# A hybrid decoder layer on one core: scan banks per kind, and steps of the planner moved

## The reference

```python
# A: gated DeltaNet, 4 heads x 128: short convolution, silu, chunked delta rule
qkv = silu(short_conv([q_a, k_a, v_a], conv_w))
v_new = u_i - w_i @ state
o     = q_i @ state + a_i @ v_new
state = state * gl + k_i.T @ v_new
# B: 4 heads x 64 over a latent of 128; a ReLU indexer of 8 heads selects 256 keys
score = sum_j relu(q_idx_j @ k_idx) * w_j ;  idx = top_k(score, 256)
p     = softmax(q_abs @ c[idx] * 64**-0.5 - slope * dist)
# C: cross-attention, 4 heads x 64, into 256 memory tokens
p_m   = softmax(q_m @ k_m * 64**-0.5) ;  o_m = p_m @ v_m
y     = concat(rmsnorm(o_a) * silu(z_a), o_s * silu(z_s), o_m * silu(z_m)) @ w_out
x     = layernorm(2**0.25 * x + y)
```

## Time and profile before

| what | us |
|---|---|
| median of 3 runs (780.77 to 781.71) | 781.16 |
| profiled execution | 782.2 |
| its span | 780.4 |
| PE busy | 712.9 (91%) |
| DVE busy | 483.9 (62%) |
| ACT busy | 452.2 (58%) |
| POOL busy | 181.7 (23%) |

### The profile page before, as it was taken

How to read it: one execution, slowest core, us unless ns; L and a number is a source line. 1 busy time by engine, 2 the same in 40 slices (tenths; PEclk the granted TensorE clock), 3 DMA queues, 4 the chain that set the end, 5 groups by cost and what they waited for, 6 DMA issues and landing times.

```text
span 780.4 us, 11927 instructions
## 1 busy us (share of the span) xinstructions
PE 712.9 (91%) x4204; PEld 591.0 (76%) x4204; DVE 483.9 (62%) x1076; ACT 452.2 (58%) x1027; POOL 181.7 (23%) x272
## 2 busy tenths in 40 slices
PE   6999999989999999999999989998777989899994
PEld 4887888778788888887888778876566767686773
DVE  5532888966756757563755658686644465654643
ACT  5522777787869987799959962223752242423410
POOL 0000000045102621136102431010365343143330
PEclk9999999999999999999999999999978999999998
DMA  9411020122300340023300252010961231332101
GB/s 356 133 68 63 19 95 29 40 72 63 120 28 29 92 136 28 28 72 89 122 28 28 85 142 83 28 47 33 333 181 40 75 115 47 109 97 74 68 28 55
DMA packets 63915, 65.90 MB, mean 84 GB/s; under 512 B 16368, under 2 KB 49392, under 8 KB 63472
## 3 DMA queue, kind: packets, MB, share of 16 engines
q1 hardware_dynamic: 63856, 65.13, 25.7%
HBM read 48.35 MB, written 16.78 MB: 83 GB/s over the span
## 4 chain that ended last, share of the span: by engine, by line
PE 63%; DVE 13%; ACT 11%; issue 9%; POOL 2%; DMA 2%; SPq 0%; ACTq 0%; DVEq 0%; POOLq 0%
PE bank L1054 10%; PE bank L1056 10%; PE bank L1055 10%; ACT cst L1938 4%; PE bank L1046 4%; PE bank L1408 4%; PE bank L1060 3%; PE bank L1409 3%; PE bank L1410 3%; DVE score L1534 2%; PE bank L1350 2%; PE bank L1240 2%; PE bank L1238 2%; PE bank L1219 2%; POOL w_out_lo L2194 2%
## 5 line engine op out<-in xcount | busy, mean ns | idle before, releaser
L1054 PE MATMUL bank<-x_hi,ring_split 128*128 128x512 f32 x480 | 197.1, 411 | 8.3 <-DVE x_lo L1483 7.3
L1056 PE MATMUL bank<-x_hi,ring_split 128*128 128x512 f32 x480 | 188.4, 393 | 0.0
L1055 PE MATMUL bank<-x_lo,ring_split 128*128 128x512 f32 x480 | 187.9, 392 | 0.0
L1938 ACT ACTIVATE cst<-score,sel 128x896 bf16<-128x896 f32 (+3 forms) x192 | 167.1, 873 | 25.7 <-DVE sel L1556 23.6
L1054 PEld LDWEIGHTS bank<-x_hi,ring_split 128*128 128x128 f32 x480 | 90.8, 189 | 25.3 <-DVE ring_split L1487 7.8
L1056 PEld LDWEIGHTS bank<-x_hi,ring_split 128*128 128x128 f32 x480 | 90.5, 189 | 19.8
L1055 PEld LDWEIGHTS bank<-x_lo,ring_split 128*128 128x128 f32 x480 | 90.9, 189 | 15.0
L1855 ACT ACTIVATE arena<-bank 128x512 f32<-128x512 f32 (+1 forms) x69 | 37.4, 563 | 55.7 <-PE bank L1060 48.6
L2125 POOL TENSOR_TENSOR arena<-arena,hsc 128x512 f32<-128x512 f32 x8 | 8.3, 1039 | 259.4 <-ACT arena L2008 259.4
L1408 PE MATMUL bank<-w_out_hi,mix_hi 128*128 128x512 f32 x128 | 54.4, 425 | 11.4 <-DVE mix_lo L1801 7.8
L2112 POOL TENSOR_TENSOR arena<-arena,cst 128x512 f32<-128x512 f32 x24 | 33.3, 1409 | 92.9 <-PE bank L1219 50.3
(11 more groups left out here) (288 smaller groups left out, 1400.9 us busy)
## 6 DMA issues: line engine op xcount, KB each, us to landing
ring<-in_w_groups SPq DMA_DIRECT2D x30, 512.0 KB, 3.4
x_raw<-in_x_t SPq DMA_DIRECT2D x8, 512.0 KB, 9.3
side_z<-stage SPq DMA_DIRECT2D x16, 256.0 KB, 2.0
w_out_sb<-in_wout_t SPq DMA_DIRECT2D x2, 2048.0 KB, 11.5
zgT<-side_z SPq DMA_DIRECT2D x8, 512.0 KB, 4.5
qkvT<-in_x SPq DMA_DIRECT2D x8, 512.0 KB, 3.4
out_y<-arena SPq DMA_DIRECT2D x8, 512.0 KB, 3.0
ring<-in_wmem_t SPq DMA_DIRECT2D x2, 1024.0 KB, 4.7
```

The source lines that it names most:

```text
L1054: nc.tensor.matmul(dst, hi, xh, start=(c == 0), stop=False)
L1055: nc.tensor.matmul(dst, hi, xl, start=False, stop=False)
L1056: last = nc.tensor.matmul(dst, lo, xh, start=False, stop=(c == KT - 1))
L1938: sc.activation(signs[order[e] % 2][:, 0:w], score[:, score_at(b):score_at(b + 1)], ACT.Sign, scale=-1.0, bias=candidate[:, b - 2:b - 1], ...
```

## The change

It is made in the planner and in the table of PSUM pools; beside them only the convolution is cut in two.

- Pools: V has bank 4, S bank 5, the outputs (R) banks 6 and 7. Other tiles of pool D still take the banks 4 to 7 in turn.
- Convolutions: a `conv` step does two of the four taps, and the second half stands one unit later, or at the start of the next list of units.
- The preparation of head 0: `KBT` stands one unit later, the product two, `latent_scale` and `base` one in the list of shares.
- Attention blocks: `norms` leaves the middle of a block and stands directly ahead of `memory`. `msc` of the next block stands one place earlier in its list, from the second block on. `mix_split(b, 1)` stands directly behind `mixT(b, 1)`, with empty units behind both.

```diff
--- before.py
+++ after.py
@@ -187,8 +187,11 @@
         units[1] = [*second, *units[1]]
         units[3] = [*fourth, *units[3]]
         if part < 2:
-            units[3].append(("conv", h, part, 0))
-            units[7].append(("conv", h, part, 1))
+            units[3].append(("conv", h, part, 0, 0))
+            units[4].append(("conv", h, part, 0, 1))
+            units[7].append(("conv", h, part, 1, 0))
+        if part == 0:
+            units[0].append(("conv", h, 1, 1, 1))
         return units
 
     def value_part(h, rest):
@@ -198,7 +201,7 @@
 
     def head(h, rest):
 
-        return [*part_of(h, 1), *part_of(h, 0, [("silu", h, 1)]), [("silu", h, 0)], *value_part(h, rest)]
+        return [*part_of(h, 1), *part_of(h, 0, [("silu", h, 1)]), [("conv", h, 0, 1, 1), ("silu", h, 0)], *value_part(h, rest)]
 
 
     side = [[("side", g, t, s)] for g in range(N_SIDE) for t in range(2) for s in range(4)]
@@ -210,7 +213,7 @@
     queries[0].append(("gate_values",))
     queries[3] += [("tok", 0, a, 1) for a in range(2)]
     queries[6].append(("ksum", 0))
-    first_work = [*keys, [("kmT",)], [("gates",)], *queries, [("gate_sums",)], [("vm",)], [("silu", 0, 0)], []]
+    first_work = [*keys, [("kmT",)], [("gates",)], *queries, [("conv", 0, 0, 1, 1), ("gate_sums",)], [("vm",)], [("silu", 0, 0)], []]
     n_units = len(first_work)
     index_tiles = [("idx", b, j, c) for b in range(2, NB) for c in range(len(idx_chunks(b))) for j in range(IXH)]
     for i, e in enumerate(index_tiles):
@@ -280,7 +283,7 @@
     def product(h):
         return [*pair("U", h), ("diag_out", h)]
 
-    ahead = [*pair("GB", 0), 1, ("KB", 0, 0), ("KB", 0, 1), 1, 1, *pair("KBT", 0), 1, 1, *product(0), *[1] * 5, ("latent_scale",), ("base", 0), *[1] * 6, ("diag_back", 0), 2]
+    ahead = [*pair("GB", 0), 1, ("KB", 0, 0), ("KB", 0, 1), 1, 1, 1, *pair("KBT", 0), 1, 1, 1, *product(0), *[1] * 4, ("latent_scale",), ("base", 0), *[1] * 5, ("diag_back", 0), 2]
     woven(ahead, value_part(0, side[:N_SIDE_AHEAD]))
     side = side[N_SIDE_AHEAD:]
     for h in range(DNH):
@@ -330,7 +333,6 @@
         units = [[("mpT", b, 0)], [("mpT", b, 1)], *[[("pT", b, k)] for k in range(b + 1)]]
         units[min(3, b + 2)].append(("rinv", b))
         units += [[] for _ in range(max(0, 5 - len(units)))]
-        units[min(5, len(units) - 1)].append(("norms", b))
         for j in range(b // 2):
             units[min(2 * j + 5, len(units) - 1)].append(("weighted", b, j))
         return units
@@ -339,6 +341,8 @@
 
         s0 = 2 * i
         pieces = [[("y", b, c, s0 + s)] for c in range(2) for s in range(2)]
+        if i:
+            return [[("mixT", b, i), ("mix_split", b, i)], [], [], [], [], *pieces]
         return [[("mixT", b, i)], [("mix_split", b, i)], [], [], *pieces]
 
     def merged(*queues):
@@ -362,13 +366,13 @@
         if nb is not None:
             at = [scores(nb, h) for h in range(SAH)]
             at[1] = [*at[1], *([("qsplit", BLOCK_ORDER[n + 2])] if n + 2 < NB else [])]
-            place = 3 if n else 4
+            place = 2 if n else 4
             at[place:place] = [[("msc", nb, 0), ("msc", nb, 1)]]
             queues.append((0.5, at))
         if n == 1:
             before = half_out(prev, 0)
             after = half_out(prev, 1)
-            out = [*before[:2], *after[:2], *[[("y", prev, c, s)] for c in range(2) for s in range(4)]]
+            out = [*before[:2], after[0], [], *[[("y", prev, c, s)] for c in range(2) for s in range(4)]]
         elif n:
             out = half_out(prev, 1)
         else:
@@ -393,6 +397,7 @@
         for unit in held[:1]:
             for e in unit:
                 add(e)
+        add(("norms", b))
         add(("memory", b))
         add(("weighted", b, b // 2))
         if n == 0:
@@ -405,7 +410,7 @@
     assert plan.index(("scanS", DNH - 2, NB - 1)) < plan.index(("reach", 7))
     assert plan.index(("At", DNH - 1, 1)) < plan.index(("dm", SELECT_ORDER[0], 1))
     assert plan.index(("tok", DNH - 1, 1, 2)) < plan.index(("dm", SELECT_ORDER[0], 2))
-    assert all(plan.index(("At", h - 1, 1)) < plan.index(("conv", h, 1, 0)) for h in range(1, DNH))
+    assert all(plan.index(("At", h - 1, 1)) < plan.index(("conv", h, 1, 0, 0)) for h in range(1, DNH))
     assert all(plan.index(("silu", h, 1)) < plan.index(("tok", h, 0, 1)) for h in range(DNH))
     return with_splits(plan)
 
@@ -478,9 +483,9 @@
     if k == "y":
         return [("Y", e[:3])] if e[3] == 0 else []
     if k == "scanV":
-        return [("D", ("V", e[1], e[2]))]
+        return [("V", ("V", e[1], e[2]))]
     if k == "scanS":
-        return [("D", ("S", e[1], e[2]))] * (e[2] < NB - 1) + [("D", ("O", e[1], e[2]))]
+        return [("S", ("S", e[1], e[2]))] * (e[2] < NB - 1) + [("R", ("O", e[1], e[2]))]
     if k == "tok":
         return [("L" if e[3] == 1 else "D", e)]
     return [(POOL_OF[k], e)] if k in POOL_OF else []
@@ -703,7 +708,7 @@
         bst, mv, rstd, ealog = hsc[:, 0:12], hsc[:, 12:14], hsc[:, 14:15], misc[:, 52:56]
         ss_k, ln_k, rs_k, f_kb, f_kd = (hsc[:, 16 + 8 * i:24 + 8 * i] for i in range(5))
 
-        pools = {"P": (0, 1), "L": (2, 3), "D": (4, 5, 6, 7), "A": (4, 5, 6), "O": (0,), "Y": (1, 7)}
+        pools = {"P": (0, 1), "L": (2, 3), "D": (4, 5, 6, 7), "V": (4,), "S": (5,), "R": (6, 7), "A": (4, 5, 6), "O": (0,), "Y": (1, 7)}
         banks = [ctx.enter_context(nc.psum_tensor(f"bank{i}", [P, 512], F32)) for i in range(8)]
         filled_sem = [sem(f"filled{i}") for i in range(8)]
         released_sem = [sem(f"released{i}") for i in range(8)]
@@ -1629,16 +1634,16 @@
                                                       ALU.mult, ALU.subtract)
                     last.then_inc(release_of(e), 1)
                 elif k == "conv":
-                    h, part, t = e[1:]
-
-                    dve.wait_ge(*released(("proj", h, part, t)))
-                    if (h, part, t) == (0, 1, 0):
-                        dve.wait_ge(cw_sem, 16)
-                    if t == 0 and part == 0 and h > 1:
-                        dve.wait_ge(*filled(("O", h - 2, NB - 1)))
-                    if t == 0 and part == 1 and h:
-                        dve.wait_ge(*filled(("At", h - 1, 1)))
-                    for j in range(4):
+                    h, part, t, half = e[1:]
+                    if half == 0:
+                        dve.wait_ge(*released(("proj", h, part, t)))
+                        if (h, part, t) == (0, 1, 0):
+                            dve.wait_ge(cw_sem, 16)
+                        if t == 0 and part == 0 and h > 1:
+                            dve.wait_ge(*filled(("O", h - 2, NB - 1)))
+                        if t == 0 and part == 1 and h:
+                            dve.wait_ge(*filled(("At", h - 1, 1)))
+                    for j in (2 * half, 2 * half + 1):
                         conv_tap(h, part, t, j)
                 elif k == "tap":
                     h, t, j = e[1:]
```

## The result

The changed kernel takes **775.82 us** (median of 4, 775.74 to 777.49) against 781.43 (median of 4) for the kernel before: a ratio of 0.9928, 95% interval 0.9914 to 0.9942. The forecast was 771.9 in a range of 764.9 to 778.0: the sign and the range held, but of the 9.3 us forecast only 5.6 came. The profiled execution's span is 774.1 us, 6.3 less than before.

What follows compares the result with a forecast made beforehand. PE was taken to bound the kernel (63% of the last-ending chain), with only its idle waits to win. Terms 1.2 + 0.7 + 0.5 - 1.1 + 2.0 + 3.3 + 2.75 - 0.1 = 9.25 us gave 771.9 us, range 764.9 to 778.0.

Steps and rivals of the forecast that it cites:

- Banks per kind, the sites: Scans: V no longer waits for the outputs' addition, 0.52 us a site; 0.5 in head 0, none in heads 1, 2.
- At(2,1): Second attention tile of head 2 waits for its new bank, last used by head 1's outputs: a loss of 1.1 us.
- Key products: Head 0 before the first scan: products a point on, latent scaling after the taps; gain 1.2 us, between 0 and 2.6.
- Convolutions: Halved, two taps go behind M's subtraction at 214 us: gain 0.7 us; nothing in later heads or during index scores.
- The whole to 466 us: Key products 1.2, convolutions 0.7 and head 0's bank site 0.5, less 1.1 at At(2,1): 1.3 us net.
- Block 3 and head 3: Norms at the first block's end (1.5 us or more) and head 3's scan (1.7), capped together by a side load: 2.0 us.
- Block 4: Second block: earlier memory scores fill the wait for POOL's low weights, norms at the end; gain 3.3 us.
- Blocks 2, 5, 1, 6, 0, 7: Same edits in later blocks, against DVE's queue: gains 1.8, 1.8, -0.9, 1.25, -1.2 and 0, sum +2.75 us.
- the neighbours: Low half directly behind the gate: saves output-product waits but delays score maxima where two-chunk blocks follow; sum -0.1 us.
- The low clock: After longer waits in blocks 1 and 0, PE's clock falls from 614 to 770 us: up to 786 us; chance 0.06.
- Rival B: The key search absorbs the first half's gains, 2.4 us less: 774.3 us; chance 0.10.

Runs made afterwards that it cites:

- experiment 8: Changed kernel with head 0's key products, latent scaling and base chain back at their old places: 778.8 us, ratio 0.9947 to the kernel before.
- experiment 5: The changed kernel run once more, unaltered, as reference of its group: 777.2 us, ratio 0.9934 to the kernel before.
- experiment 3: Changed kernel with the attention blocks ordered as before; only scan banks, key products and convolutions remain: 781.6 us, ratio 0.9994.
- experiment 9: Changed kernel with the memory scores of the next block at their old place: 783.0 us, ratio 1.0018.
- experiment 10: Changed kernel with norms in the middle of each block as before: 774.5 us, ratio 0.9906.
- experiment 7: Changed kernel with another bank for At(2,1); for blocks 1 and 0, memory scores at their old place and the preceding block's gate and low half apart: 775.2 us.
- experiment 12: Kernel of experiment 11 with head 0's key products back at their old places: 773.3 us, ratio 0.9899.
- experiment 4: Changed kernel with gate and low half apart again, as before: 778.3 us, ratio 0.9943.
- experiment 6: Changed kernel with At(2,1) of head 2 in bank 5 and not 7, second run of that kernel: 777.8 us, ratio 0.9943.
- experiment 11: Kernel of experiment 7 with norms of blocks 1 and 0 in the middle again, these two blocks wholly as before: 772.9 us, ratio 0.9887.
- experiment 2: Kernel before with the attention blocks' edits alone: 779.8 us, ratio 0.9965.

## Why the prediction was right, and where its sizes were off

- **Banks per kind, the sites.** In each scan of heads 0 to 2 the ladder wins 0.4 us and loses it again by the next head's M or first copies: 0.1 lasts in head 0, where I counted 0.5 (mis-sized), and nothing in heads 1 and 2, as forecast. Head 3: 1.7 forecast, 1.3 by the ladder (+1.6 to +0.3).
- **At(2,1).** The mechanism and the place were right, the term was mis-sized: 1.1 us forecast, 1.7 measured, of which 1.4 last. I had worked it out from PE's position in the kernel before, 1.1 us ahead of the release. The release moves with PE, but not by all of it: the 0.4 us that the banks win in the scan just ahead bring PE on and not the addition, which ended 1.4 us earlier where PE was 1.8 earlier. 1.1 and 0.4 are the 1.5 us of all seven profiles; the rest lies between the end of the addition (370.08) and PE's start (370.23).
- **Key products.** 1.2 us forecast, 1.4 measured (+1.1 at 159 us to -0.3 at 200; experiment 8 gives 1.5). Right, and for the reason given: 2.1 us won by 188, and the rest taken back by the search, at 195 us already and not at 206. The base chain came late in no profile: no M waited for it.
- **Convolutions.** This step failed. The 0.7 us at M came (0.9, -0.3 to -1.2), but I had put the halves at nothing while the index scores run, "the same work in another order", and they cost 0.8 us there. Before 123 us DVE had room for those taps without holding PE; a few microseconds later ACT and then PE wait for it. That the sum of DVE's work stays the same says nothing on that, and I had not looked at where DVE had room. Net 0.1 in place of 0.7.
- The whole to 466 us: forecast 1.3 us net. Measured 0.3 behind from the loads, 1.4 and 0.1 won, 0.1 in head 0's scan, 1.4 lost at At(2,1): a loss of 0.1 us, 0 by the ladder.
- **Block 3 and head 3.** 2.0 forecast; 2.7 in this trace from 470 to the last product of block 3, 2.2 in experiment 5. Head 3's scan gives 1.3 of it. Norms at the end gives nothing (experiments 3, 9 and 10). From 551 us to y(3,0,0) experiment 3, whose blocks stand in the order of before, wins 0.9 us as well: in the profile of the kernel before the clock was at 1.2 GHz without a break from 563.5 to 573.7 us, in experiment 3 from 567.7 to 571.1. So some 0.9 us of this term seem to belong to that one execution of the kernel before; the rest stays open.
- **Block 4.** 3.3 forecast, 4.0 measured: PE's wait for the low half of 0.9 us didn't come, one of 0.50 did. In experiments 5, 7, 10 and 12 it is 3.0, since there the clock fell right behind the wait for POOL's low weights; in the first profile, and in experiments 4, 6, 8 and 11, it fell at 581 to 583 us instead, where it cost nothing in the end, for PE then waited only 1.2 us for these weights and not 2.56.
- **Blocks 2, 5, 1, 6, 0, 7** with the neighbours: forecast -1.4, -2.4, +1.5, -1.5, +1.6, -0.45, measured -1.4, -2.4, +1.5, -0.7, +1.8, 0. Counting DVE's queue instruction by instruction from the last output product gave four of six to 0.2 us, though in blocks 1 and 0 the wait stood at the scores and not at y. Block 6's low half was late by 0.87 us at y(6,0,0), which the forecast had not.
- **The low clock.** 1.6 us at 465, which the forecast had only as a case of 6%, in the blocks and for all of them at once. It comes one stretch at a time, and in one execution of a kernel and not in the next. Experiments 2, 5 and 6 show it in block 1 as well.

9.25 forecast less 1.3 (first half), plus 0.7 (block 3), plus 0.7 (block 4), less 1.5 (the rest), less 1.6 (clock) is 6.3, the difference of the spans. The medians differ by 5.6, since the profiled execution of before was 0.8 above its median and that of the changed kernel was on its own. Three causes of about equal size, the first half, the later blocks and the clock, cost 4.4 us of the forecast; 1.4 us came in its favour in blocks 3 and 4, and these are luck as far as the two bullets above show: they hang on where the clock was low in the two profiled executions. Rival B (the search absorbs 2.4 us, which would have left a loss of 1.1 at 466 us) is nearest for the first half, but the search took back only 0.7; a bank and DVE's queue under the index scores took the rest. Without the place of the memory scores nothing is left of the gain in time (experiment 9).

## What to carry to other kernels

When a tile moves behind a reader on another engine, the wait is that reader's release less PE's position after all the other edits, and an engine whose queue follows PE releases earlier when PE is earlier: here the wait was 1.5 us in seven profiles, whatever PE had won before. Work moved later in a queue can cost though its sum stays the same, here 0.8 us: look at what stands behind its new place. Where a planner's edit is good for most blocks and bad for two, count the queue of the engine behind it for each block and make the edit per block; together with the bank of At(2,1) that turned 5.6 us into about 9. And read a change of a few tenths of a per cent by the starts of paired instructions, since executions of one kernel moved by up to 8 us. Then read the clock of both traces before a lead is put down to an edit: the block that seemed to win 1.0 us by norms did so by a stretch of low clock that stood elsewhere.

## What was not expected of the hardware

PE's granted clock fell after waits of 2.01 to 2.07 us at 195 us in five of five profiles, after 1.73 to 1.83 us in none of four, after 1.91 to 1.93 us at 466 us in four of eleven; and after 0.79 to 1.08 us in none of four. In block 3 one and the same wait of 1.82 to 1.86 us for the low half was followed by it in six of twelve profiles; in the other six PE then waited 2.56 us for POOL's low weights, and it fell after that in all six. A fall cost from nothing, where PE had to wait for another engine behind it anyway, to 1.6 us. The Trainium skill ("TensorE: Matmul & The Clock Gate", "HAM oscillation — how this bites in real kernels") describes kernels in which TensorE's clock falls after its waits again and again; here the same wait in the same kernel was followed by a low clock in one execution and not in the next (466 us, the changed kernel and experiment 5). Whether the waits cause it, or another thing that both go with, wasn't tried.
